# Dealt modulation products, four PSUM homes for late units, plain probability transposes and a late softmax scaling

## What is computed

```python
mod = silu(c) @ w_ada + b_ada                  # 9 conditioning rows, 6 x 1024 columns
sh1, sc1, g1, sh2, sc2, g2 = split(mod, 6)
h = (rms_norm(x, g) * (1 + sc1) + sh1) @ w_in  # q, k, v of two mixers and an indexer
# mixer A: 8 heads under three dilated windows; mixer B: 8 heads over the top 256 keys of the indexer
p = exp(s - max(s));  l = sum(p);  o = (p / l) @ v
y = x + g1 * (o @ w_out);  y = y + g2 * swiglu(rms_norm(y) * (1 + sc2) + sh2)
```

## Time and profile before

| | us |
|---|---|
| median of three runs | 1939.26 (1938.38 to 1940.05) |
| the profiled execution | 1938.74 |
| its span | 1937.1 |
| busy in the span: PE, DVE, ACT, POOL | 1755.0, 944.3, 668.4, 535.5 |
| mean granted TensorE clock | 0.95 of 2.4 GHz |

### The profile page before, as it was taken

One profiled execution on the slowest core, in us unless ns is written; L12 is line 12 of the kernel. 1 busy time (PEld: TensorE's weight loads), 2 busy tenths in 40 slices (PEclk: granted clock), 3 DMA queues, 4 the chain that ended last, 5 costly groups with the idle time before them and its releaser, 6 DMA issues. The chain is left out here.

```text
span 1937.1 us, 30827 instructions
## 1 busy us (share of the span) xinstructions
PE 1755.0 (91%) x11234; PEld 1607.0 (83%) x11234; DVE 944.3 (49%) x2225; ACT 668.4 (35%) x1784; POOL 535.5 (28%) x661
## 2 busy tenths in 40 slices
PE   6697778989984999999878989999999999999998
PEld 4495367877873788888848979999999999999998
DVE  2705697887894677777643162232133033123124
ACT  4415423321321888888713233111111111211111
POOL 0334234541453222121012205223222222321310
PEclk8898799999996999999988999999999999999999
DMA  7600013344214112110055012112111111111002
GB/s 232 231 23 13 5 42 113 105 132 138 78 56 133 65 55 88 33 62 1 5 200 198 23 44 69 57 28 64 44 32 54 43 43 43 43 43 43 22 1 90
DMA packets 137907, 135.37 MB, mean 70 GB/s; under 512 B 7085, under 2 KB 126813, under 8 KB 137158
## 3 DMA queue, kind: packets, MB, share of 16 engines
q1 hardware_dynamic: 136150, 131.07, 21.3%
q0 software_dynamic: 1648, 2.89, 0.5%
HBM read 115.29 MB, written 27.04 MB: 73 GB/s over the span
## 5 line engine op out<-in xcount | busy, mean ns | idle before, releaser
L2424 DVE TENSOR_TENSOR hf<-bank,sg 128x352 f32<-128x352 f32 x66 | 34.6, 525 | 464.9 <-PE bank L2172 455.3
L2172 PE MATMUL bank<-ahi,gwh 128*128 128x352 f32 x1056 | 196.2, 327 | 11.3 <-DVE hf L2424 6.7
L2333 POOL TENSOR_TENSOR hlo<-hf,hhi 128x352 fp32r<-128x352 f32 x66 | 62.7, 949 | 505.1 <-ACT hhi L2262 505.1
L2437 DVE SCALAR_TENSOR_TENSOR x<-wide,modT,x 128x352 f32<-128x352 f32 (+1 forms) x264 | 151.3, 573 | 96.8 <-PE wide L2188 96.8
L2172 PE MATMUL bank<-alo,gwh 128*128 128x352 f32 x1056 | 192.6, 324 | 2.0 <-DVE alo L2413 2.0
L2172 PE MATMUL bank<-ahi,gwl 128*128 128x352 f32 x1056 | 194.2, 326 | 0.0
L2172 PEld LDWEIGHTS bank<-ahi,gwh 128*128 128x128 f32 x1056 | 176.2, 190 | 14.0 <-DVE hf L2424 7.0
L1164 DVE TENSOR_SCALAR_CACHE_REDUCE junk<-sig,cand 128x896 uint8<-128x896 f32 (+6 forms) x217 | 177.8, 878 | 0.6
L2172 PEld LDWEIGHTS bank<-alo,gwh 128*128 128x128 f32 x1056 | 174.9, 189 | 2.7 <-DVE alo L2413 2.7
L2172 PEld LDWEIGHTS bank<-ahi,gwl 128*128 128x128 f32 x1056 | 176.5, 191 | 0.0
L1526 PE MATMUL bank<-diag,prob 128*128 128x128 f32 x1152 | 167.1, 282 | 5.4 <-ACT diag L1662 4.7
(11 more groups left out here) (298 smaller groups left out, 3443.6 us busy)
## 6 DMA issues: line engine op xcount, KB each, us to landing
raw<-in_w_ada SPq DMA_DIRECT2D x24, 1024.0 KB, 5.4
gw<-in_w_gate_up SPq DMA_DIRECT2D x44, 512.0 KB, 5.1
raw<-in_w_in SPq DMA_DIRECT2D x11, 1024.0 KB, 5.7
dw<-in_w_down SPq DMA_DIRECT2D x22, 512.0 KB, 3.6
scr_x<-xT SPq DMA_DIRECT2D x1, 4224.0 KB, 16.2
xnat<-in_x_prompt SPq DMA_DIRECT2D x8, 512.0 KB, 5.6
scr_q<-ubuf SPq DMA_DIRECT2D x32, 128.0 KB
qn<-scr_q SPq DMA_DIRECT2D x8, 512.0 KB, 3.9
```

The source lines that it names most:

```text
L2172: mm = pe.matmul(pb[2 * s + side][:, 0:THIRD], a[r][:, k, side, :], b[:, k, third(th)], start=(p == 0 and k == 0), stop=(p == 2 and k == K ...
L2333: pool.tensor_tensor(hlo[:, r, third(th)], hf[:, (3 * r + th) % 2, :], hhi[:, r, third(th)].bitcast(F32), ALU.subtract).then_inc(h_lo, 1)
L2424: v.tensor_tensor(hf[:, s, :], pb[2 * s + 1][:, 0:THIRD], sg[:, s, :], ALU.mult).then_inc(h_mul, 1)
L2437: ins = v.scalar_tensor_tensor(out=x1[:, d, cols], in0=src[:, 0:n], scalar=modT[:, 40 + d, 0:1], in1=x1[:, d, cols], op0=ALU.mult, op1=ALU ...
```

## The change

It does four things.

1. **Modulation.** `cT` is padded with zeros to 32 columns, so that the eight k slices can be dealt over four strips of 32 PSUM partitions, two slices each; ScalarE copies all 128 partitions, and the turn is now an ordinary product with a constant `modsel` (128 x 9), which adds the four strips as it turns. In the late part the products alternate between two banks, their turns wait until a unit of the next projection is done, and the bias is added by ScalarE.
2. **Late units** go round four PSUM homes: banks 0 and 1 and the two halves of `wide[0]`.
3. **Attention.** Probabilities are turned plainly, with the identity. The diagonal and the inversion in each step are gone; all 16 x 8 row sums are kept.
4. **sample_attention** inverts the sums, GpSimd repeats each inverse over its head's 64 columns, TensorE turns that, and VectorE multiplies the attention's output by it, in 16 pieces of 128 x 512, between the steps of the eight sequences. GpSimd's loads of value pages stand behind the repeats in its queue.

```diff
-    ada_bank = [(bank[0], bank[1]) if a < ada_at else (bank[2], bank[3]) for a in range(len(adas))]
+    ada_bank = [(bank[0], bank[1]) if a < ada_at else (bank[2 + a % 2], wide[1][:, 512 * (a % 2):512 * (a % 2) + 512])
+                for a in range(len(adas))]
+    late_bank = [bank[0], bank[1], wide[0][:, 0:512], wide[0][:, 512:1024]]
+    def unit_bank(u):
+        return bank[u % 2] if u < NIDX else late_bank[(u - NIDX) % 4]
...
-                    mm = pe.matmul(ada_bank[a][0][0:9, 0:WCH], cT[:, k, :], raw[:, n % 3, k, :],
-                                   start=(k == 0), stop=(k == KD - 1))
+                    j = 32 * (k % 4)
+                    mm = pe.matmul(ada_bank[a][0][j:j + 32, 0:WCH], cT[:, k, :], raw[:, n % 3, k, :],
+                                   start=(k < 4), stop=(k >= 4))
...
-                    mm = pe.transpose(ada_bank[a][1][:, j * 9:j * 9 + 9], modn[:, a % 2, j * P:(j + 1) * P],
-                                      ident[0:9, 0:9])
+                    mm = pe.matmul(ada_bank[a][1][:, j * 9:j * 9 + 9], modn[:, a % 2, j * P:(j + 1) * P],
+                                   modsel[:], start=True, stop=True)
...
-            def project(n):
+            def project(n, turns=()):
...
                     mm.then_inc(unit_mm, 1)
+                    if t < len(turns):
+                        ada_turn(turns[t])
...
+            def ada_bias(a):
+                act.wait_ge(ada_tr, a + 1)
+                for j in range(2):
+                    last = act.activation(modT[:, 2 * a + j, :], ada_bank[a][1][:, 9 * j:9 * j + 9], ACT.Identity,
+                                          bias=vecT[:, 2 * a + j:2 * a + j + 1])
+                last.then_inc(ada_done, 1)
...
-                        mm = pe.matmul(dst[:, (j - 4 * b) * P:(j - 4 * b + 1) * P],
-                                       prob[:, a % RING, j * P:(j + 1) * P], diag[:, a % 4, :],
-                                       start=True, stop=True)
+                        mm = pe.transpose(dst[:, (j - 4 * b) * P:(j - 4 * b + 1) * P],
+                                          prob[:, a % RING, j * P:(j + 1) * P], ident[:])
...
-                    act.activation(diag[:, m % 4, :], ident[:], ACT.Copy,
-                                   scale=rinv[:, m % 4:m % 4 + 1]).then_inc(diag_in, 1)
...
-                    v.reciprocal(rinv[:, m:m + 1], rowsum[:, m:m + 1]).then_inc(r_sum, 1)
...
+            pool.wait_ge(inv, 1)
+            for u in range(16):
+                p, g = divmod(u, 2)
+                if u >= 4:
+                    pool.wait_ge(spread, u - 3)
+                pool.tensor_copy(rexp[:, u % 4], rinv[:, 2 * p:2 * p + 2, 4 * g:4 * g + 4]
+                                 .rearrange("p h t -> p t h").unsqueeze(3).to_broadcast([P, 4, 2, HD])
+                                 ).then_inc(widened, 1)
...
+            def spread_inverse(u):
+                pe.wait_ge(widened, u + 1)
+                if u == 0:
+                    pe.wait_ge(qe, 1)
+                else:
+                    pe.wait_ge(scaled, u)
+                for j in range(4):
+                    mm = pe.transpose(bank[0][:, j * P:(j + 1) * P],
+                                      rexp[:, u % 4, j].rearrange("p h d -> p (h d)"), ident[:])
+                mm.then_inc(spread, 1)
...
+            def scale_rows(u):
+                p, g = divmod(u, 2)
+                v.wait_ge(spread, u + 1)
+                v.tensor_tensor(oT[:, p, 512 * g:512 * g + 512], oT[:, p, 512 * g:512 * g + 512], bank[0][:],
+                                ALU.mult).then_inc(scaled, 1)
```

More of the change, by code:

```diff
@@ L117, in constants @@
     c["pick"] = pick
+    c["modsel"] = (row[:, None] % 32 == np.arange(9)[None]).astype(np.float32)
     c["headsel"] = (h[:, None] == np.arange(8)[None]).astype(np.float32)
@@ L178, in front @@
     gains = T.at("gains", [P, 4, HD], F32, T.end)
-    cT = T.at("cT", [P, KD, 9], F32, T.end)
+    cT = T.at("cT", [P, KD, 32], F32, T.end)
+    modsel = T.at("modsel", [P, 9], F32, T.end)
     sc1 = T.at("sc1", [P, KD, 9], F32, T.end)
@@ L202, in front @@
     valid = T.at("valid", [NSAMP, NEWW], F32, T.end)
-    modn = T.at("modn", [9, 2, WCH], F32, T.end)
-    assert T.end <= 24576, T.end
-    XB = 24576
+    modn = T.at("modn", [P, 2, WCH], F32, T.end)
+    assert T.end <= 25344, T.end
+    XB = 25344
     xhi = T.at("xhi", [P, KD, 1152], F32R, XB)
@@ L691, in _ @@
             indexer()
-            turn = None
+            turns = []
             for n in range(ada_at + 3, len(order)):
                 if n in ada_no:
-                    if turn is None:
+                    if ada_no[n] == ada_at:
                         pe.wait_ge(ix_acc, 49)
                     ada(n)
-                    turn = ada_no[n]
-                    ada_turn(turn)
-                else:
-                    project(n)
+                    turns.append(ada_no[n])
+                else:
+                    project(n, turns)
+                    turns = []
+            for a in turns:
+                ada_turn(a)
         @block.scalar
@@ L859, in _ @@
                         root(u - 1)
+                        if turns:
+                            ada_bias(turns.pop(0))
                         if t == SPLIT_AT and pj.index(n) + 1 < len(pj):
@@ L862, in _ @@
             root(len(units) - 1)
+            for a in turns:
+                ada_bias(a)
         @block.gpsimd
@@ L867, in _ @@
             pool.memset(xhi[:, :, TOK:1152].bitcast(F32), 0.0)
+            pool.memset(cT[:], 0.0)
             pool.memset(xlo[:, :, TOK:1152].bitcast(F32), 0.0).then_inc(pads, 1)
@@ L1766, in sample_attention @@
     rsum = T.at("rsum_s", [P, 4], F32, T.end)
+    rexp = T.at("rexp", [P, 4, 4, 2, HD], F32, T.end)
     n_pool = A["cache_k"].shape[1]
     assert T.end <= S["loaded"]
+    rowsum, rinv = S["rowsum"], S["rinv"]
     ldc = sem("s_consts")
+    inv = sem("s_row_inverse")
+    spread = sem("s_inverse_spread")
+    scaled = sem("s_rows_scaled")
+    widened = sem("s_inverse_widened")
     k_in = [sem(f"s_k_in{r}") for r in range(3)]
@@ L1927, in _ @@
         def _(v):
+            v.reciprocal(rinv[:], rowsum[:]).then_inc(inv, 1)
+            def scale_rows(u):
[3 more added lines that the diff above has]
+                                ALU.mult).then_inc(scaled, 1)
             v.wait_ge(zero, 1)
```

66 lines of the change are left out of this document (32 added, 34 removed).

## The result

The changed kernel takes 1876.05 us (median of four runs, 1875.41 to 1876.41) against 1938.82 before: a ratio of 0.9676, 95% interval 0.966 to 0.9693. The profiled execution went from a span of 1937.1 to 1874.3 us. The gain is 62.8 us where 85 was forecast.

The account below looks back on a forecast made before the run. Only the four stages before the feed-forward part can change, with VectorE binding late and three engines almost level in the attention: 1938.7 - 10 - 44 - 50 + 19 = 1853.7, with the half microsecond 1854 us, range 1817 to 1890.

Parts of the forecast that it names:

- the rival in which the attention stays hand-to-hand: Attention takes 300 instead of 277 us, or late part gains 20 instead of 44; about 1878 us, chance 0.16.
- an attention over 300 us: Attention: a sign that the forecast is wrong; some 277 us was the sign that it is right.
- longer waits of ScalarE for stores: Late part: a sign that the forecast is wrong, ScalarE waiting on stores longer than before the change.
- What bounds: Whole kernel: the 921 us from the feed-forward part's start stay; any gain or loss lies in the four stages before.
- Dealt product and turn: Modulation: product 1.2 us instead of 3.62, turn 0.47 instead of 0.35; early gain 10 us, ends 0 and 19.
- Late part: Late projections: VectorE binds, waits of 43.1 us and biases of 2.8 go, 4 given back; gain 44 us, ends 20 and 50.
- Attention: Attention: 68 us leave TensorE, leaving 244; stage takes 277 us, a gain of 50; ends 244 and 327.
- an 88% taken from the late part: Attention: TensorE's 244 us divided by the late part's busy share, 309 of 352 us, gives 277 us.
- The slow rival: Attention: transposes do not hold the clock up, TensorE's 244 us become 488 at 1.2 GHz; kernel 2065 us, chance 0.05.
- Sample stage: Sample stage: scaling moved into it adds 19 us, ends 8 and 30; first value product some 55 us after stage start.
- one of its two paths: Sample stage, 19 us more: sequences and score groups take 37 against 17.8 us; or late page loads delay the value products.
- the zigzag: Sample stage: each sequence one chain of transposes, copies and multiplication, about 4.0 us; eight are 32 us.

Follow-up runs that it names:

- b1: The changed kernel with the modulation product left in one column strip, eight steps after one another, no summing over strips: 1890.4 us.
- a4: The changed kernel with the rounding of queries and keys for the next head moved from ScalarE to GpSimd: 1858.6 us.
- a1: The kernel before with only the attention and sample-stage edits: 1917.7 us.
- a2: The kernel before with only the edits ahead of the attention: 1892.1 us.

## Why the prediction was right, and where it was short

The forecast was faster, 1854 in 1817 to 1890; 1876 came. The direction and the stages are right. But 1876 lies just above the 1835 to 1875 that had most of the weight, next to the 1878 of the rival in which the attention stays hand-to-hand, and two of the forecast's own signs of being wrong came: an attention over 300 us (301.5) and longer waits of ScalarE for stores (146 us against 63). Point by point:

- **What bounds.** Right: nothing behind the barrier moved by more than 1.3 us.
- **Dealt product and turn.** Right: 1.07 and 0.51 us against 1.2 and 0.47. Early it gave all of the 7.6 us (b1 loses them), where 10 was forecast. The three products ahead of the fourth gave nothing, not 4: the fourth starts at 46.11, before at 46.18. The other five bring the last bias forward by 5.9 us (to 61.8 from 67.7), as forecast (6). The first projection gains only 4.5 (71.19 instead of 75.65): behind that bias a VectorE step takes 4.42 us instead of 0.23 beside a GpSimd step (shown at the end), and ScalarE waits 2 us for it before it makes the operands. Its row above names GpSimd's split of the weights, but the part that it needs is done by 66.2.
- **Late part.** The mechanism was right: VectorE binds, and the waits of the earlier trace rows fell from 43.1 to 6.5. Three sizes were off. Waits of 6.5 us stay where 4 were given back, and the removal of 2.8 us of biases was outweighed by 5.2 us more in two small search steps, which the forecast held constant. Behind the last search step 4 us went, not 2. ScalarE's longer waits for stores cost little here: VectorE stays at 96%.
- **Attention.** This is the term that was mis-sized: -34, not -50, between the forecast and the 27 of the rival in which it stays hand-to-hand. The work that left was right (70 us on TensorE against 68; ScalarE and VectorE to 242 and 228 for the whole stage). The step that failed is the one that divided TensorE's 244 us by an 88% taken from the late part. The share that came, 85% at a clock of 0.99, is so near by luck, for nothing in the late part says how these engines meet; it accounts for 10 of the missing 16 us and the clock for 6. The engines are level over the stage but not within a head: ScalarE's longest exponential, eight evictions and the roundings for the next head fall into one half, most of TensorE's long scores and value products into the other. The forecast named that place ("ScalarE at a head's first steps") and gave it no time. a4 took 18 us of copies out of it and came to 283.4 us at the clock that the forecast kept, 52 less than before.
- **Clock in the attention.** The slow rival (2065 us) is out: the mean granted clock is 0.97, so TensorE ran at 2.4 GHz for nearly all of the stage. The 0.99 that the forecast kept was still 6 us too good. The Trainium skill's rule ("TensorE: Matmul & The Clock Gate", section "PE-mode transpose"), by which transposes don't engage the full clock, does not hold here in the form that the rival gave it.
- **Sample stage.** Right to 0.1 us in size, and by one of its two paths. Cut as the forecast cut it, from the first window turn to the second group of scores, the eight sequences take 31.8 us (895.92 to 927.71) and not 37, so the zigzag adds 14 us. The page loads set the end: the first value product starts 56 us after the last one of the attention (884.4 to 940.9; forecast some 55), and the 5.09 us in which it waits for them (1.60 us for another load before) make up most of the rest. A widening took 0.61 us on GpSimd, below the lower bound of 0.65.

## What to carry over

When an edit brings several engines to the same sum over a stage, don't divide the largest sum by a busy share: cut one period of the loop into stretches, take the fuller engine in each, and add those. Then move work out of the stretch where an engine is full, not off the engine that has the largest total. Where several edits take away the same wait, undoing one shows only what the others don't cover (here 3 to 8 of 34 us). Lend a buffer only from when it is free. And before you take a row's word for what ended a wait, look at when the step that it names was done.

## What the runs showed that was not expected

**The clock falls inside a loop whose code does not change.** Three neighbouring stretches of the changed kernel's attention (columns as above):

```profile
620.00:625.00 5.00, 3.39 (x27) 2.93 (x25) 2.97 (x11) 4.82 (x14) 3.76 (x3) 1.00 0.00 0
625.00:630.00 5.00, 4.31 (x16) 3.18 (x15) 2.85 (x8) 3.29 (x8) 0.28 (x1) 0.66 0.00 0
630.00:635.00 5.00, 5.00 (x37) 4.45 (x36) 3.77 (x8) 2.25 (x6) 0.00 (x0) 1.00 0.00 0
```

After a half in which TensorE was idle a third of the time, part of the next stretch ran at 1.2 GHz. The same half 20 us later was followed by no fall, and a1's profile has none behind the first 7 us of the stage. Whether the idle time or the share of transposes in that half lets the clock fall, no run tells apart.

**A small VectorE step waits out a GpSimd step.** VectorE's and GpSimd's timelines after, late:

```profile
458.17 0.73 DVE L1204 SCALAR_TENSOR_TENSOR cand<-nok,cand 128x7 uint32<-128x7 uint32 x1
466.17 0.17 DVE L1204 SCALAR_TENSOR_TENSOR cand<-nok,cand 128x7 uint32<-128x7 uint32 x1
...
484.71 0.73 DVE L1204 SCALAR_TENSOR_TENSOR cand<-nok,cand 128x7 uint32<-128x7 uint32 x1
```

```profile
484.68 0.73 POOL L931 TENSOR_TENSOR ubuf<-ubuf,gains 128x256 f32<-128x256 f32 x1 [1.95 <-DVE ubuf L1252]
```

Of the 31 executions of L1204, 14 overlap no GpSimd step and take 0.17 us each; the 17 that do take 0.71 to 0.73. Before, also 17 overlapped, but several only in part (0.58 on average). At the start, the step behind the last early bias and GpSimd's first two splits of weights, in the changed kernel, then in a2 with the same code there:

```profile
61.84 4.42 DVE L1059 SCALAR_TENSOR_TENSOR sc<-modT,vecT 128x72 f32<-128x72 f32 x1
61.67 8.96 POOL L907 TENSOR_TENSOR wlo<-raw,whi 128x2048 fp32r<-128x2048 f32 x2 [58.97 <-ACT whi L755]
```

```profile
60.94 0.23 DVE L1059 SCALAR_TENSOR_TENSOR sc<-modT,vecT 128x72 f32<-128x72 f32 x1
61.28 9.40 POOL L907 TENSOR_TENSOR wlo<-raw,whi 128x2048 fp32r<-128x2048 f32 x2 [58.58 <-ACT whi L755]
```

Over all fourteen profiles: in the six in which this step starts at least 0.2 us before the split, it takes 0.23 us; in the eight in which it starts with the split or after it, 4.3 to 4.6. Six of VectorE's late scalings stretch in the same way, before and after, from 0.43 to 3.3 us each: 17 us of the engine that binds there. The Trainium skill ("GPSIMD Engine Reference", section "1. Specifications") says that GpSimd's SBUF interfaces are shared with VectorE, with contention when a VectorE instruction has two SBUF inputs; these rows agree. No run moved GpSimd's split away on purpose to see what that is worth.
